# Where the high and low halves of the operands start in SBUF, and the order of the first loads, in a two-block transformer kernel

## What is computed

```
z  = rmsnorm(x, g_mix) @ w_in            # and the latent, rotary and gated attention parts
x += attention parts @ w_o
u  = relu(rmsnorm(x, g_mlp) @ w_up);  x += (u * u) @ w_down          # 1024 -> 4096 -> 1024
x += sigmoid(rmsnorm(x, g_ple) @ w_ple_gate) * (p @ w_ple)
for layer in 0, 1:                        # second block
    x += 0.5 * swiglu(rmsnorm(x), w_in, w_out)      # 1024 -> 2 x 2816 -> 1024, four times in all
    x += mixer(rmsnorm(x))                # layer 0: gated linear + forget attention; 1: sparse latent attention
    x += 0.5 * swiglu(rmsnorm(x), w_in, w_out)
out = rmsnorm(x, final_norm_g_2)
```

## Time and profile before

| | |
|---|---|
| median of 3 runs | 1387.79 us (1387.4 to 1388.41) |
| profiled execution: its own time | 1387.96 us |
| profiled execution: span from first to last instruction | 1385.9 us |
| TensorE busy with matmuls | 1350.8 us, 97% of the span |
| TensorE weight loads | 1164.1 us |
| VectorE, ScalarE, GpSimd busy | 974.1, 677.7, 70.3 us |
| mean DMA rate | 174 GB/s |
| mean granted TensorE clock | 0.99 of full |

### The profile page before, as it was taken

One profiled execution on the slowest core, in us unless ns is written; L12 is line 12 of the kernel. 1 busy time (PEld: TensorE's weight loads), 2 busy tenths in 40 slices (PEclk: granted clock), 3 DMA queues, 4 the chain that ended last, 5 costly groups with the idle time before them and its releaser, 6 DMA issues.

```text
span 1385.9 us, 19410 instructions
## 1 busy us (share of the span) xinstructions
PE 1350.8 (97%) x7680; PEld 1164.1 (84%) x7680; DVE 974.1 (70%) x1328; ACT 677.7 (49%) x1057; POOL 70.3 (5%) x109
## 2 busy tenths in 40 slices
PE   8999999999999999999999999999999988999998
PEld 6988988888888888897788888888888776888886
DVE  5886777666688767658577676777666697577665
ACT  6576454443565444455554444444444456444442
POOL 0300010000000000003000000000000033000000
PEclk9999999999999999999999999999999999999999
DMA  8433546556546555454346655465654453466551
GB/s 311 154 123 122 175 174 229 183 184 195 168 154 218 193 189 188 158 182 126 120 151 212 194 192 191 162 203 198 197 183 149 150 176 86 140 205 210 190 183 46
DMA packets 67738, 241.31 MB, mean 174 GB/s; under 512 B 8015, under 2 KB 8408, under 8 KB 67648
## 3 DMA queue, kind: packets, MB, share of 16 engines
q1 hardware_dynamic: 65344, 234.19, 50.9%
q0 software_dynamic: 2016, 5.77, 1.7%
q10 hardware_dynamic: 288, 0.11, 0.0%
HBM read 238.88 MB, written 1.09 MB: 173 GB/s over the span
## 4 chain that ended last, share of the span: by engine, by line
PE 88%; DVE 6%; ACT 2%; issue 2%; DMA 1%; POOL 1%; DVEq 0%; ACTq 0%; POOLq 0%
PE pp L461 86%; PE pp L470 2%; DVE wlo L1682 2%; DVE fa L1682 1%; DVE hx L1690 1%; ACT whi L1237 1%; ACT pbuf L1388 1%; DVE pbuf L1686 1%; DMA gns<-gains 0%; ACT hx L1238 0%; ACT xn L1276 0%; DVE fa L1679 0%; DVE X L1690 0%; DVE xn L1891 0%; DMA fa<-t_rows 0%
## 5 line engine op out<-in xcount | busy, mean ns | idle before, releaser
L1682 DVE TENSOR_TENSOR wlo<-raw,whi 128x1024 fp32r<-128x1024 f32 (+1 forms) x445 | 522.9, 1217 | 149.9 <-ACT whi L1237 149.6
L461 PE MATMUL pp<-hx,whi 128*128 128x512 f32 (+1 forms) x2400 | 543.9, 362 | 7.5 <-DVE fa L1682 3.6
L461 PEld LDWEIGHTS pp<-hx,whi 128*128 128x128 f32 x2400 | 425.8, 191 | 76.8 <-issue 7.1
L1237 ACT ACTIVATE whi<-raw 128x1024 fp32r<-128x1024 f32 (+1 forms) x445 | 441.9, 1041 | 97.2 <-PE pp L461 88.6
L461 PE MATMUL pp<-whi,ra 128*128 128x512 f32 x1144 | 366.1, 391 | 0.0
L461 PE MATMUL pp<-hx,wlo 128*128 128x256 f32 x2032 | 323.3, 283 | 0.0
L461 PEld LDWEIGHTS pp<-hx,wlo 128*128 128x128 f32 x2032 | 287.0, 192 | 9.0
L461 PEld LDWEIGHTS pp<-whi,ra 128*128 128x128 f32 x1144 | 214.8, 188 | 43.9 <-issue 0.9
L461 PE MATMUL pp<-wlo,ra 128*128 128x512 f32 x572 | 222.8, 390 | 0.0
L1782 DVE TENSOR_REDUCE fa<-pp 128x512 f32<-128x1024 f32 x104 | 127.0, 1221 | 76.5 <-PE pp L461 76.5
L1237 ACT ACTIVATE ra<-fa 128x512 fp32r<-128x512 f32 x63 | 39.9, 633 | 228.3 <-DVE fa L1690 228.3
(11 more groups left out here) (175 smaller groups left out, 780.0 us busy)
## 6 DMA issues: line engine op xcount, KB each, us to landing
raw<-w_chunks SPq DMA_DIRECT2D x437, 512.0 KB, 5.2
fa<-t_rows POOLq DMA_DIRECT2D x16, 128.0 KB, 3.6
raw<-w_chunks SPq DMA_DIRECT2D x5, 256.0 KB, 6.1
fx<-x_t SPq DMA_DIRECT2D x2, 512.0 KB, 4.7
X<-x_in SPq DMA_DIRECT2D x2, 512.0 KB, 8.3
fa<-g_fin POOLq DMA_DIRECT2D x2, 512.0 KB, 5.0
fa<-f_rows POOLq DMA_DIRECT2D x8, 128.0 KB, 3.2
cst<-consts POOLq DMA_DIRECT2D x1, 576.0 KB, 7.4
```

The source lines that it names most:

```text
L461: return pe.matmul(o, lhs, rhs, start=first, stop=last, skip_group_check=True)
L1237: return act.activation(o, i, ACT.Copy, scale=1.0)
L1682: return dve.tensor_tensor(o, a, b, op)
```

## The change

**Addresses.** `wlo` is allocated ahead of `whi`, with 64 bytes between them; `ra` grows by 240 columns. In the built program `wlo` now starts at 18432, `whi` at 51264, `hx` at 84032, `ra` at 100416 and `raw` at 117760. So `whi`, `hx` (high and low halves) and the high halves in `ra` start 64 bytes behind a multiple of 512, and `wlo` and the low halves in `ra` on a multiple. No instruction of the steady stages is added, removed or moved.

**Head.** ScalarE issues the gains before the constants, and the constants have a semaphore of their own, which TensorE and GpSimd wait for later. The first chunk comes in pieces of 512, 512 and 1024 columns.

```diff
@@ -169,8 +169,8 @@
         n = sum(p[3] for p in pieces)
-        step = HW // 2 if i == 0 else HW
-        halves += [(i, c, min(step, n - c)) for c in range(0, n, step)]
+        cuts = [0, HW // 2, HW, n] if i == 0 else [*range(0, n, HW), n]
+        halves += [(i, c, e - c) for c, e in zip(cuts, cuts[1:])]
         HEND.append(len(halves))
@@ -199,10 +199,11 @@
         sb("pad", [128, 120])
+        wlo = sb("wlo", [128, NHL, CW], R)
+        sb("pad_hi", [128, 16])
         whi = sb("whi", [128, NHL, CW], R)
-        wlo = sb("wlo", [128, NHL, CW], R)
         hx = sb("hx", [128, 8, 2, S], R)
-        ra = sb("ra", [128, 4096], R)
+        ra = sb("ra", [128, 4336], R)
         raw = sb("raw", [128, NRAW, HW])
@@ -218,7 +219,7 @@
         s_raw = [sem(f"s_raw{i}") for i in range(NRAW)]
-        s_x = sem("s_x")
+        s_x, s_ident = sem("s_x"), sem("s_ident")
         s_xt = [sem(f"s_xt{i}") for i in range(2)]
@@ -316,9 +317,9 @@
         cqh = rar(0, 512).rearrange("p (k c) -> p k c", k=2)
-        cql = rar(512, 512).rearrange("p (k c) -> p k c", k=2)
-        ckh = rar(1024, 256).rearrange("p (k c) -> p k c", k=1)
-        ckl = rar(1280, 256).rearrange("p (k c) -> p k c", k=1)
+        cql = rar(624, 512).rearrange("p (k c) -> p k c", k=2)
+        ckh = rar(1152, 256).rearrange("p (k c) -> p k c", k=1)
+        ckl = rar(1520, 256).rearrange("p (k c) -> p k c", k=1)
         ZB = [[4, 6], [5, 7]]
@@ -327,18 +328,18 @@
         oh = rar(0, 2048).rearrange("p (k c) -> p k c", k=8)
-        ol = rar(2048, 2048).rearrange("p (k c) -> p k c", k=8)
+        ol = rar(2160, 2048).rearrange("p (k c) -> p k c", k=8)
         ma = far(2368, 1024).rearrange("p (s c) -> p s c", s=2)
...
         uh = rar(0, 1536).rearrange("p (s c) -> p s c", s=3)
-        ul = rar(1536, 1536).rearrange("p (s c) -> p s c", s=3)
+        ul = rar(1648, 1536).rearrange("p (s c) -> p s c", s=3)
         fr = far(0, 1024).rearrange("p (s c) -> p s c", s=2)
...
         gf = far(4096, 1024)
-        ph = rar(3072, 512).rearrange("p (k c) -> p k c", k=2)
-        pl = rar(3584, 512).rearrange("p (k c) -> p k c", k=2)
+        ph = rar(3200, 512).rearrange("p (k c) -> p k c", k=2)
+        pl = rar(3824, 512).rearrange("p (k c) -> p k c", k=2)
         gs = far(0, 2048).rearrange("p (t d) -> p t d", t=2)
@@ -371,7 +372,7 @@
         mh = rar(0, 2048).rearrange("p (k c) -> p k c", k=8)
-        ml = rar(2048, 2048).rearrange("p (k c) -> p k c", k=8)
+        ml = rar(2160, 2048).rearrange("p (k c) -> p k c", k=8)
         gov = go.rearrange("p (r s c) -> p s r c", r=2, s=2)
@@ -393,7 +394,7 @@
         ch = rar(0, 512).rearrange("p (k c) -> p k c", k=2)
-        cl = rar(512, 512).rearrange("p (k c) -> p k c", k=2)
+        cl = rar(624, 512).rearrange("p (k c) -> p k c", k=2)
         OFF, KL = (0, 128), (128, 256)
@@ -785,7 +786,7 @@
                     pe.wait_ge(s_hl, n + 1)
-                    pe.wait_ge(s_lo, n + 1)
+                    pe.wait_ge(s_lo, min(n + 1, 3))
                     a = 512 * n
@@ -799,6 +800,7 @@
                 pe.wait_ge(s_in, 32)
+                pe.wait_ge(s_ident, 16)
                 spread(0, 2)
@@ -1411,17 +1413,17 @@
                 n = CONST["tri"][0]
-                act.dma_start(cst[:, 0:n], CST[:, 0:n]).then_inc(s_first, 16)
                 act.dma_start(gns[:, :], GNS).then_inc(s_first, 16)
+                act.dma_start(cst[:, 0:n], CST[:, 0:n]).then_inc(s_ident, 16)
                 act.wait_ge(s_warm, 1)
                 copy(pb[:, 512:1024], pb[:, 0:512])
-                act.wait_ge(s_first, 32)
+                act.wait_ge(s_first, 16)
                 gain = G("g_mix")
...
                     copy(hh[:, k, :], xT[:, k, :], scale=gain[:, k:k + 1]).then_inc(s_hh)
-                    if k < 4:
+                    if k < 3:
                         split_half()
@@ -1933,13 +1935,13 @@
                 dve.memset(pb[:, 0:512], 0.0).then_inc(s_warm)
-                dve.wait_ge(s_first, 32)
+                dve.wait_ge(s_first, 16)
                 gain = G("g_mix")
...
                          ALU.subtract).then_inc(s_hl)
-                    if k < 4:
+                    if k < 3:
                         split_half()
@@ -2348,8 +2350,8 @@
                 n, m = CONST["tri"][0], CONST["hot"][0]
-                pool.wait_ge(s_first, 32)
-                pool.wait_ge(s_lo, 6)
+                pool.wait_ge(s_ident, 16)
+                pool.wait_ge(s_lo, 5)
                 pool.dma_start(cst[:, n:m], CST[:, n:m]).then_inc(s_in, 16)
@@ -2483,12 +2485,11 @@
                 load(j)
-            load(5)
             sp.dma_start(fx[:, 1024:2048], XT[1]).then_inc(s_xt[1], 16)
             for c in range(2):
-                load(6 + c)
+                load(5 + c)
                 sp.dma_start(X[:, :, 512 * c:512 * c + 512], xv[:, :, 512 * c:512 * c + 512]).then_inc(s_x, 16)
-            for j in range(8, len(halves)):
+            for j in range(7, len(halves)):
                 load(j)
...
             sp.dma_start(ov[:, 0, :], X[:, 0, :]).then_inc(s_out, 16)```

SyncE's queue at the start of the program, before the change (`raw` is the ring of weight pieces, `fx` the transposed input, `X` the input):

```order
L2483 DMA fx<-x_t 128x1024
L2479 DMA raw<-w_chunks 128x512 x4
L2479 DMA raw<-w_chunks 128x1024
L2479 DMA raw<-w_chunks 128x1024 [waits s_lo]
L2487 DMA fx<-x_t 128x1024
L2479 DMA raw<-w_chunks 128x1024 [waits s_lo]
```

## The result

The changed kernel is slower by 0.33% (0.19% to 0.46%), though the forecast was faster.

What follows compares the result with a forecast made beforehand. The prediction took TensorE's matmul pitch as the bound: 1387.96 us less 0.5 for the head and 3.4 for the changed pairs gave 1384.1, less 0.17 over the median 1383.9, stated as 1383.8 us, range 1368 to 1394.

Steps and rivals of the forecast that it cites:

- What bounds the kernel: Whole kernel: TensorE, busy 97% of the span, sets the time by its pitch from one matmul to the next.
- The changed pairs: About 2032 pairs, nearly all 256-column, get another load-stream distance and gain 1.9 ns each: 3.9 us, 3.4 on the chain.
- For the pairs shifted together no row shows anything but 227 and 120 ns, so I take no change: Pairs whose load and stream move by the same bytes, 512-column shapes among them: pitch unchanged, 0 us.
- The bound for a loss: Pairs shifted together: at worst the 230 ns of a high batch's first six matmuls.
- The "slower" rival: 512-column batches stay at 230 ns instead of 227: 10.9 us, 9.6 on the chain, giving 1393.6 to 1397 us; chance 0.19.
- point of decision: A 512-column pitch rise of 1.2 ns, from which the slower case decides against the gains of 3.4 and 0.5 us.
- The rule of the two ports: Skill page: TensorE has separate read ports for moving operand and weight loads, so addresses would be worth 0 us.
- addresses do nothing: Rival: low batches settle at 120.0 ns again, only the head gains, 1387.3 us; chance 0.29.
- The head: Kernel start: gains land earlier, the weight piece is late next, TensorE starts about 0.65 us earlier; taken as 0.5 us.
- by itself ... shortens nothing: Head: filling the DMA gap of 8.0 to 10.5 keeps weights ahead of TensorE but by itself gains nothing.
- 1383.9 rounded to 1383.8: Last step of the sum: 1384.1 less 0.17 gave 1383.9 us, stated as 1383.8.
- up to a second: Head: cost named for the wider third piece if its split were not hidden; it was taken as hidden.

Runs made afterwards that it cites:

- w64: `head_only` with both weight halves, `whi` and `wlo`, moved 64 bytes off the grid of 512, `hx` and `ra` on it; 1385.59 us, ratio 0.9981 to the kernel before.
- wlo64: `head_only` with `wlo` alone moved 64 bytes off the grid of 512; 1393.76 us, ratio 1.0047 to the kernel before.
- all64: `head_only` with all matmul operands moved together by 64 bytes; 1385.38 us, ratio 0.9984 to the kernel before.
- loads_alternate: `head_only` with only the low halves in `ra` moved, to 64 bytes ahead of the grid; 1388.71 us in one run.
- addr_only: The kernel before with the new addresses and its old head; 1393.45 us, ratio 1.0047 to the kernel before.
- head_only: The changed kernel with the addresses of the kernel before, so only the new head; 1385.43 us, ratio 0.9987 to the kernel before.
- hx192: `head_only` with `hx` alone moved by 192 bytes; 1381.69 us, ratio 0.9964 to the kernel before.
- ra_low64: The changed kernel with the low halves in `ra` at 64 too, so `wlo` alone stays on the grid; 1389.41 us, ratio 1.0020 to the kernel before.
- hx64: `head_only` with `hx` alone moved 64 bytes off the grid of 512; 1381.91 us, ratio 0.9951 to the kernel before.
- hx256: `head_only` with `hx` alone moved by 256 bytes; 1384.06 us in one run.

## Why the prediction was wrong

- **What bounds the kernel** was right: TensorE before and after, and the time goes by its pitch.
- **The changed pairs** (-3.4 us) came out right in size. The low batches stand at 117.6 ns against the foretold 118.1. Measured: -3.7 us, and -0.6 in the other 256-column shape. That the rows gave the number is partly luck: in "small" and "kwi" the load is off the grid and the stream on it, in the changed low batches it is the other way round, and the runs show that sign and neighbours matter: with the load at 64 and the stream at 0, `w64` has 114.1 ns and `wlo64` 118.0.
- **"For the pairs shifted together no row shows anything but 227 and 120 ns, so I take no change"** is the step that failed. It put the 512-column shapes at nothing, and they lost 12.1 us in sum: the down and output projections went from 227.5 to 233.5 and from 228.1 to 232.1 ns, 8.9 us, the high batches from 227.8 to 229.3, 2.5 us, and the first mixer 0.7 us. The step looked only at the distance inside a pair. `all64` shows where it holds: if all operands move together and stay, nothing changes. `loads_alternate` and `wlo64` show where it breaks: when the start changes from one matmul to the next, the loads alone cost 2.0 and 3.6 ns, the streams alone 3.8 and 4.5 (with a small share of the distance in one pair of three), and both at once 6.0 and 3.9 ns. The high batches fit this only in part: inside them nothing alternates, and their loss is larger behind a low batch, whose loads start at 0 (2.0 ns a step), than behind a down projection (1.2). The rows could not show it, since before the change nothing alternated in the 512-column shapes.
- **The bound for a loss**, 230 ns from the first six matmuls of a high batch, was too low for the down projections, and held for the high batches on average, which still settle at 227 ns, only later. The "slower" rival put 3 ns on all 3624 matmuls; measured are 6.0 and 4.0 ns on 1704 of them and 1.5 to 2 on the others. Its point of decision, 1.2 ns on the mean, was passed: the mean over the 3624 rose by 12.1 us / 3624 = 3.3 ns.
- **The rule of the two ports.** Pitches of 113 to 120 ns for 256 columns and of 227 to 234 ns for 512, from instructions that differ in start addresses alone, mean that "addresses do nothing" is refuted: `addr_only` is slower with its whole interval above 1.003. The Trainium skill, page "SBUF — State Buffer", section "Who interferes with whom", says that PE never waits on anyone; the measurement decides against a reading of it by which the two reads of TensorE's own don't disturb each other.
- **The head.** The order of events was right: the weight piece was late next (landed at 6.78), the first real matmul stands at 8.30 (foretold 8.5), and the hole in the DMA was filled (387 GB/s against 168). The term, 0.5 us, was mis-sized: 1.7 us in the trace, 1.8 us by `head_only`. Of the steps behind it, the one that the runs contradict is that the filled gap "by itself ... shortens nothing". With the clock at full from 12.4 us on, the old order of loads leaves TensorE waiting for weights (`addr_only`), and the new one does not (`head_only`). In the changed kernel the clock did rise earlier, with 7 more matmuls between 9.14 and 14.65, but the runs do not tie that to the start of the work: the old head in `addr_only` had it too, and with the same new head the granted clock of 8.00 to 10.50 and of 10.50 to 13.50 us was 0.50 and 0.90 in `hx192`, 0.87 and 0.54 in `ra_low64`, and 1.00 in both in `all64` and `hx64`. How the 1.8 us divide between the parts of the head stays open.
- **Slips in the sum.** 1383.9 rounded to 1383.8 is not a rounding, and "up to a second" for the wider third piece can't be meant as it stands, since the whole program takes 1.4 thousandths of one. Neither changes the outcome.

What stays open: why a distance of 64 bytes lets a low batch run at 113 ns behind one neighbour and at 118 behind another, why 512-column batches pay for a distance that 256-column batches gain from, and how the reads of stream and load meet inside SBUF or TensorE. The runs give the rule of the pitches, not the mechanism.

## What to carry to other kernels

Where TensorE is the bound, read the pitch from starts in the time line, for each shape, and list the start addresses modulo 256 of stream and load for three matmuls in a row, not for one pair: an operand whose start changes from one matmul to the next cost 2 to 6 ns of 227 here, even with stream and load kept together. A shift of the activations alone against all weights, 64 bytes, is worth trying (here 0.9951 of the time, of which the new head alone has 0.9987), with each shape measured, since short streams gained and long ones lost. That operands are shifted together is no ground for "no change" without a row that shows it.

## What the runs showed of the hardware

- The pitch of float32r matmuls with 128 x 128 weights depends on the start addresses of the moving and the stationary operand: 113 to 120 ns for 256 columns, 227.3 to 233.5 ns for 512.
- The pattern repeats with 256 bytes (`hx256` as `head_only`, `hx192` as `w64`), and a shift of all operands by 64 bytes changes nothing (`all64`).
- In 512-column matmuls a constant distance of load minus stream of 64 costs 5.5 to 6 ns, one of -64 0.8 to 1.9 (`w64`, `hx64`).
- Starts that alternate cost 2.0 to 3.6 ns a matmul in the loads alone (`loads_alternate`), 3.8 to 4.5 in the streams alone (`wlo64`), each with one pair in three at a distance of 64, and 3.9 to 6.0 ns in both with no distance at all (`addr_only`).
- The same batch with the same addresses runs at 113.1 or at 118.1 ns, by what stands before it.
- TensorE's clock at full from 12.4 us instead of 14.65 gained nothing with the old order of loads (the first 148 matmuls end at 39.83 us in `addr_only`, 39.54 before, with some 0.2 us for the addresses), and 1.6 us with the new one (37.95 in `head_only`).
